# Expert units of the first table from 58 on: token halves side by side in 512-column products, summed by VectorE before the gelu

## What is computed

```
def peer_ffn(h, w_q, sub_keys, u_tab, v_tab):
    ...
    def expert_chunk(args):
        hx, ix, gx = args
        u = u_tab[ix]
        act = jax.nn.gelu(jnp.einsum('chkd,cd->chk', u, hx).astype(jnp.float32))
        vv = v_tab[ix]
        return jnp.einsum('chk,chkd->cd', (gx * act).astype(vv.dtype), vv)
```

## Time and profile before

| what | us |
|---|---|
| median of 3 runs | 2144.68 |
| the profiled execution, own time | 2145.49 |
| its span | 2144.2 |
| PE busy (share of the span) | 2113.1 (99%) |
| DVE busy | 1395.7 (65%) |
| ACT busy | 1247.4 (58%) |
| POOL busy | 977.1 (46%) |
| first table on PE, first and last start | 357.0 to 786.9 |

### The profile page before, as it was taken

One profiled execution on the slowest core, in us unless ns is written; L12 is line 12 of the kernel. 1 busy time (PEld: TensorE's weight loads), 2 busy tenths in 40 slices (PEclk: granted clock), 3 DMA queues, 4 the chain that ended last, 5 costly groups with the idle time before them and its releaser, 6 DMA issues.

```text
span 2144.2 us, 37243 instructions
## 1 busy us (share of the span) xinstructions
PE 2113.1 (99%) x14292; PEld 1958.1 (91%) x14292; DVE 1395.7 (65%) x2706; ACT 1247.4 (58%) x2272; POOL 977.1 (46%) x791
## 2 busy tenths in 40 slices
PE   7999999999999999999999999999999999999999
PEld 7999989999999998888889899998888999998887
DVE  4467655998676756666667765557764864757874
ACT  5669454546777865455445465746555465756553
POOL 4776557999667650000004785660001876661000
PEclk9999999999999999999999999999999999999999
DMA  6444565655444456666665554555565645455565
GB/s 231 149 138 129 172 197 173 196 178 180 145 140 147 141 168 204 195 192 192 195 195 196 186 157 139 155 180 167 187 205 158 189 146 168 141 165 177 187 194 160
DMA packets 103952, 370.59 MB, mean 173 GB/s; under 512 B 11480, under 2 KB 12896, under 8 KB 103264
## 3 DMA queue, kind: packets, MB, share of 16 engines
q1 hardware_dynamic: 103776, 368.21, 54.8%
HBM read 366.05 MB, written 2.11 MB: 172 GB/s over the span
## 4 chain that ended last, share of the span: by engine, by line
PE 88%; DVE 6%; ACT 2%; POOL 1%; issue 1%; DMA 1%; SPq 0%; DVEq 0%; ACTq 0%; POOLq 0%
PE stream_bank L568 14%; PE stream_bank L570 14%; PE stream_bank L569 14%; PE side_bank L568 9%; PE side_bank L570 9%; PE side_bank L569 9%; PE side_bank L577 4%; PE stream_bank L577 4%; PE side_bank L574 2%; PE stream_bank L574 2%; PE side_bank L918 1%; PE side_bank L917 1%; POOL unit_lo L2606 1%; ACT unit_hi L1181 1%; PE side_bank L746 1%
## 5 line engine op out<-in xcount | busy, mean ns | idle before, releaser
L2606 POOL TENSOR_TENSOR unit_lo<-raw,unit_hi 128x512 fp32r<-128x512 f32 (+1 forms) x724 | 938.5, 1324 | 943.6 <-ACT unit_hi L1181 941.6
L1181 ACT ACTIVATE unit_hi<-raw 128x1024 fp32r<-128x1024 f32 (+1 forms) x678 | 708.9, 1046 | 199.5 <-PE side_bank L570 66.0
L1777 DVE TENSOR_TENSOR unit_lo<-raw,unit_hi 128x1024 fp32r<-128x1024 f32 (+1 forms) x316 | 390.3, 1236 | 227.9 <-ACT unit_hi L1181 225.9
L568 PE MATMUL stream_bank<-hT,unit_hi 128*128 128x256 f32 x1360 | 398.9, 293 | 1.8 <-POOL unit_lo L2606 1.8
L570 PE MATMUL stream_bank<-hT,unit_lo 128*128 128x256 f32 x1360 | 384.6, 283 | 0.0
L569 PE MATMUL stream_bank<-hT,unit_hi 128*128 128x256 f32 x1360 | 384.5, 283 | 0.0
L568 PE MATMUL stream_bank<-h2T,unit_hi 128*128 128x256 f32 x1024 | 293.3, 286 | 0.0
L570 PE MATMUL stream_bank<-h2T,unit_lo 128*128 128x256 f32 x1024 | 289.8, 283 | 0.0
L569 PE MATMUL stream_bank<-h2T,unit_hi 128*128 128x256 f32 x1024 | 289.6, 283 | 0.0
L568 PEld LDWEIGHTS stream_bank<-hT,unit_hi 128*128 128x128 f32 x1360 | 259.9, 191 | 3.6 <-POOL unit_lo L2606 2.0
L569 PEld LDWEIGHTS stream_bank<-hT,unit_hi 128*128 128x128 f32 x1360 | 260.0, 191 | 1.6
(11 more groups left out here) (392 smaller groups left out, 4303.9 us busy)
## 6 DMA issues: line engine op xcount, KB each, us to landing
raw<-in_peer_u_dram SPq DMA_DIRECT2D x128, 512.0 KB, 3.5
raw<-in_peer_v_dram SPq DMA_DIRECT2D x128, 512.0 KB, 4.1
raw<-in_gate_dram SPq DMA_DIRECT2D x64, 512.0 KB, 3.5
raw<-in_gt_dram SPq DMA_DIRECT2D x44, 512.0 KB, 3.5
raw<-in_up_dram SPq DMA_DIRECT2D x44, 512.0 KB, 3.5
raw<-in_ffn_out_dram SPq DMA_DIRECT2D x44, 512.0 KB, 3.5
raw<-in_branch_dram SPq DMA_DIRECT2D x32, 512.0 KB, 3.5
raw<-in_w_gate_dram SPq DMA_DIRECT2D x24, 512.0 KB, 3.5
```

What stands on the lines that cost most here:

```text
L568: mm(out, l.hi, r.hi, start=start, stop=False)
L1181: activation(k.unit_hi[n % SPLIT_SLOTS][:, 0:w], k.raw[n % RAW_SLOTS][:, 0:w], ACT.Copy).then_inc(k.sem("unit_hi"), 1)
L1777: V.tensor_tensor(k.unit_lo[s][:, 0:w], k.raw[n % RAW_SLOTS][:, 0:w], k.unit_hi[s][:, 0:w], ALU.subtract).then_inc(unit_lo, 1)
L2606: last = G.tensor_tensor(k.unit_lo[s][:, cols], k.raw[n % RAW_SLOTS][:, cols], k.unit_hi[s][:, cols], ALU.subtract)
```

## The change

Units 58 to 127 of the first table go through `halves_unit`: 8 products of 512 and 8 of 256 columns. DVE has a new step `sum_unit(r)`: a reduce that reads the 512 columns of the stream bank in pairs (column t and 256+t), writes the 256 sums to the right half of the side bank `SIDE + 2 + r % 2`, and frees the stream bank. ACT's gelu of such a unit waits for this sum instead of PE and reads it; a new semaphore `unit_gelu` tells DVE that it is done. DVE's step r is put in another order: `sum_unit(r-1)`, `second_keys` of both halves, `gate_unit(r-1)`, `apply_gates`.

```diff
--- before.py
+++ after.py
@@ -172,6 +172,7 @@
 SETS, GROUP = 3, 4
 GROUPS = TOKENS // GROUP
 GATES_FROM, GATES_OVER = 55, 70
+HALVES_FROM = 58
 SLOTS_EXP, SLOTS_TURN = (21, 46), (28, 54)
 HEADS_MIXER = MEM_HEADS + Q_HEADS
 TOKEN_MAJOR = ("vm", "va", "w_out", "peer_v", "rv", "gv", "sv", "ffn_out")
@@ -922,7 +923,10 @@
         pe.wait_ge(k.sem("landed_sub_keys"), 16)
         scores(0)
         for r in range(KEYS):
-            fm_unit("peer_u", r, k.h2T, KD, ready=(lambda c: (k.sem("scaled_lo"), c // 2 + 1)) if r == 0 else None)
+            if r >= HALVES_FROM:
+                halves_unit("peer_u", r, k.h2T)
+            else:
+                fm_unit("peer_u", r, k.h2T, KD, ready=(lambda c: (k.sem("scaled_lo"), c // 2 + 1)) if r == 0 else None)
             if r == 1:
                 scores(1)
             if r in SLOTS_TURN:
@@ -1465,15 +1469,19 @@
         def evict_gated(r):
 
             b, m = k.bank_of["peer_u", r], tokens_gated(r)
-            act.wait_ge(unit_mm, U["peer_u", r] + 1)
+            src, done = k.bank[b][:, 0:TOKENS], k.free[b]
+            if r < HALVES_FROM:
+                act.wait_ge(unit_mm, U["peer_u", r] + 1)
+            else:
+                act.wait_ge(*k.over["peer_u", r])
+                src, done = k.bank[SIDE + 2 + r % 2][:, TOKENS:], k.sem("unit_gelu")
             if m:
                 if units_gated(r) > 2:
                     act.wait_ge(k.sem("unit_gated"), units_gated(r) - 2)
-                last = activation(k.bank[SIDE + 2 + r % 2][:, 0:m], k.bank[b][:, 0:m],
-                                  ACT.Gelu_apprx_tanh)
+                last = activation(k.bank[SIDE + 2 + r % 2][:, 0:m], src[:, 0:m], ACT.Gelu_apprx_tanh)
             if m < TOKENS:
-                last = activation(k.experts[:, r, m:], k.bank[b][:, m:TOKENS], ACT.Gelu_apprx_tanh)
-            last.then_inc(k.free[b], 1)
+                last = activation(k.experts[:, r, m:], src[:, m:], ACT.Gelu_apprx_tanh)
+            last.then_inc(done, 1)
 
         def expert_hi(j):
             if j == 0:
@@ -2218,13 +2226,16 @@
                                               k.slot_T[:, 2:4, t:t + 1].to_broadcast([P, 2, P]), ALU.is_equal, ALU.mult)
             last.then_inc(k.sem("second_hot"), 1)
 
+        def gelu_done(r):
+            return k.over["peer_u", r] if r < HALVES_FROM else (k.sem("unit_gelu"), r - HALVES_FROM + 1)
+
         def apply_gates(g, r):
 
             tokens = slice(g * GROUP, (g + 1) * GROUP)
             gates = k.bank[SIDE + g % 2][:, :].rearrange("p (t j) -> p j t", t=GROUP)
             dve.wait_ge(k.sem("gates_mm"), 2 * g + 2)
             V.tensor_copy(k.experts[:, r:, tokens], gates[:, r:, :])
-            dve.wait_ge(*k.over["peer_u", r - 1])
+            dve.wait_ge(*gelu_done(r - 1))
             V.tensor_tensor(k.experts[:, 0:r, tokens], k.experts[:, 0:r, tokens], gates[:, 0:r, :], ALU.mult).then_inc(
                 k.free[SIDE + g % 2], 1)
 
@@ -2233,7 +2244,7 @@
             if m == 0:
                 return
             row = k.experts[:, r, 0:m]
-            dve.wait_ge(*k.over["peer_u", r])
+            dve.wait_ge(*gelu_done(r))
             dve.wait_ge(*k.over["gates", m // GROUP - 1])
             V.tensor_tensor(row, row, k.bank[SIDE + 2 + r % 2][:, 0:m], ALU.mult).then_inc(
                 k.sem("unit_gated"), 1)
@@ -2250,15 +2261,24 @@
             cols = slice(t * P, (t + 1) * P)
             dve.wait_ge(*k.over["slots", t])
             own.then(V.tensor_tensor(k.slot_T[:, 3, cols], k.slot_T[:, 2, cols], k.gate_hi[:, cols], ALU.subtract))
+        def sum_unit(r):
+            b = k.bank_of["peer_u", r]
+            dve.wait_ge(unit_mm, U["peer_u", r] + 1)
+            V.tensor_reduce(k.bank[SIDE + 2 + r % 2][:, TOKENS:], k.bank[b][:, :].rearrange("p (a t) -> p t a", a=2), AXIS_X,
+                            ALU.add).then_inc(k.free[b], 1)
+
         for r in range(KEYS):
             advance("peer_u", r)
+            if r > HALVES_FROM:
+                sum_unit(r - 1)
+            for g in groups_built(r):
+                second_keys(g, 0)
+                second_keys(g, 1)
             if r:
                 gate_unit(r - 1)
             for g in groups_built(r - 2):
                 apply_gates(g, r)
-            for g in groups_built(r):
-                second_keys(g, 0)
-                second_keys(g, 1)
+        sum_unit(KEYS - 1)
         expert_lo(0)
         gate_unit(KEYS - 1)
         expert_lo(1)
```

## The result

The changed kernel takes 2147.32 us (median of 20 runs, 2144.68 to 2151.22) against 2142.66 us of the kernel before in the same series (20 runs, 2139.11 to 2147.41). The ratio is 1.0020, 95% interval 1.0014 to 1.0026: slower by 0.2%, 3.0 to 5.6 us. The forecast was +5.8 us (1.0027), 2150.5 us for the median, in a range of 2142.5 to 2160.

A forecast was written before the change was run, and what follows sets the result against it. PE bounds the kernel now; with the change a two-round loop through DVE and ACT was to decide. 61 x 0.11 = +6.7, 9 x -0.07 = -0.6, gaps -0.5, end +0.2: +5.8 us, median 2150.5 us, range 2142.5 to 2160.

The forecast's parts named there:

- 70 x 0.07 = 4.9 us: PE, units 58 to 127: each goes from 2.88 to 2.81 us, 4.9 us less if PE stays the bound.
- The reduce, 0.68: DVE, one reduce of 512 PSUM elements per unit: 0.68 us, from a 683 ns row; at the other end 1568 ns.
- The loop, 3.87 in the middle: Chain through PE, DVE and ACT over two rounds: 7.74 us, 3.87 a round; 3.83 early, 3.95 late.
- The gelu link: ACT, inside the loop: the gelu's two pieces, from start to the start of what follows, 0.39 us.
- The hand-over to PE: From the end of ACT's first keys to a waiting PE: 0.10 us, with 0.05 and 0.35 as ends.
- The sum, +5.8 us: Whole kernel: 61 units with a group +6.7, nine without -0.6, gaps -0.5, table's end +0.2.
- The end of the table, +0.2: Unit 127's reduce between PE's last product and the second table: +0.2 us, of at most 0.7.
- Stalls of 0.1 to 0.6 us in the waits: Sign in PE's waits: first keys (L1466) named on the gates' second half, several tens of times, 0.1 to 0.6 us each.
- The first, that all of PE's gain comes through: Rival: the loop stays shorter than PE's own round, under 3.70; 4.9 us gained less 0.2, 2140.0 us; chance 0.13.
- The second, a loop that is about even: Rival: a reduce of 0.60 and hand-overs of nothing take 0.12 off a round; 2143 to 2149 us; chance 0.23.
- a reduce of 1.0 us: Rival, DVE becomes the bound: 10 us more, 2160; chance 0.14 shared with a hand-over of 0.35, 2158.
- a PE unit that isn't shortened: Rival: PE's units gain nothing as 128-column products follow each; some 2 us more, inside the forecast's spread; no chance given.

The follow-up runs named there:

- the first experiment: The changed kernel with DVE's gate_unit and apply_gates moved between the second keys of half 0 and half 1: 2139.24 us, 0.9982 of the kernel before.
- the first two experiments: The changed kernel with gate_unit and apply_gates ahead of half 1's second keys on DVE, or half 1's first keys ahead of the gelu on ACT: 0.9982 and 0.9984.
- the reduce twice: The changed kernel with the reduce done twice in each unit, the second behind the first: 2171.25 us, 1.0131 of the kernel before.
- the reduce in the old order: The changed kernel with DVE's order of before behind the reduce, second keys of both halves last: 2148.43 us, 1.0029 of the kernel before.
- the reduce alone: The changed kernel with the old products (24 of 256 columns) in all units, the reduce reading the left half twice: 2150.65 us, 1.0036 of the kernel before.
- the order alone: The kernel before with only DVE's new order, second keys of both halves ahead of the gated rows, no reduce: 2142.89 us, 0.9999 of the kernel before.
- PE's part alone: The kernel before with units 58 to 127 as halves products, no reduce, the gelu reading the left half alone: 2137.71 us, 0.9975 of the kernel before.
- the last version: The changed kernel with gates ahead on DVE, first keys ahead on ACT, and unit 127 with old products and no reduce: 2135.91 us, 0.9973 of before.
- the second experiment: The changed kernel with the first keys of half 1 moved ahead of the gelu on ACT: 2139.81 us, 0.9984 of the kernel before.

## Why the prediction was right, and where its sizes were off

- **What bounds the kernel, and the mechanism.** Right. PE alone was the bound, and the loop half 0, second keys, gated rows, reduce, gelu, first keys, half 1 took its place. Taking the loop apart at either end gave 8.7 us back; the reduce without the products kept it; the order without the reduce had none of it. The stream of weights, which I cost at nothing, stayed covered: no view of PE's waits names a low part.
- **The term "70 x 0.07 = 4.9 us".** Measured alone 5.5 (0.079 a unit). The figures of the Trainium skill, "TensorE: Matmul & The Clock Gate", section "Wait — 56ns, not 53.3ns?", had given an estimate of 1.4; the interval of the run, 3.2 to 7.7 us less, leaves that out too.
- **The reduce, 0.68.** 0.693, with 691 to 700 ns over 70 of them. Its upper end, 1568 ns, was not near.
- **The loop, 3.87 in the middle.** It is 3.85. The passage above gives 0.04 + 1.05 + 0.82 + 0.73 (reduce and hand-over) + 0.33 + 0.75 + 0.07 = 3.79 from half 0 to the next half 1, where I had 3.87. The gelu link was mis-sized: 0.39 was read to the start of first keys that themselves had waited for PE's half 0; from the gelu's start to the next start it is 0.33. The hand-over to PE takes 0.05 to 0.07 after a short stall, not 0.10. PE's part, from half 1 at 623.44 over one unit to the modelled end of the next half 0 (627.08 + 0.27 = 627.35), is 3.91 where I had 3.87; with the loop cut, in the first experiment, the same stretch takes 3.84 to 3.88. This lengthening, about 0.04 us a round, is what the 8.7 us hold beside the late starts of 6.5 us; its cause isn't shown. 3.79 + 3.91 = 7.70 for two rounds, 3.85 each.
- **The sum, +5.8 us.** This is the step that was off: the stage gave 3.2, the runs 3.0 to 5.6. I counted 61 units with a group and 9 without, with six gaps, and six is also what the description of the kernel before says; the program leaves out five units (66, 78, 89, 101, 113), so they are 62 and 8. With these counts my prices give 62 x 3.77 + 8 x 2.88 = 256.8 us for the old stage (it is 257.0) and 62 x 3.88 + 8 x 2.81 - 0.5 = 262.5 for the new one (it is 260.2). Of the 2.3 us, 1.9 are the round, 3.85 instead of 3.88. The rest is the lead that the loop gets at each of the five gaps, larger than the 0.5 us in all that I gave: 62 x 3.85 + 8 x 2.80 = 261.1 against 260.2 measured.
- **The end of the table, +0.2.** In the changed kernel's profile PE stood 1.95 us there, 0.1 less than before; in the first two experiments 2.83, 0.8 more. See the last section.
- **Stalls of 0.1 to 0.6 us in the waits.** The stalls are there, nearly every second round, most of them 0.16 to 0.36 us long; but as waits the view shows only six, since modelled ends hide the rest. What I named as the sign of the theory was nearly absent in that view, and was found in the starts.
- **The rivals.** The first, that all of PE's gain comes through, is what the kernel does once the loop is cut; the change itself was 8.7 us away from it. The second, a loop that is about even, had 2143 to 2149 us, and the measured 2147.32 lies in that band and not in the forecast's 2149 to 2156. That is partly since the kernel before itself measured 2142.66 over 20 runs, 2.0 less than the three that I started from. Its mechanism, a reduce of 0.60 and hand-overs of nothing, isn't what the trace shows (0.69, and 0.03 to 0.07). DVE was not the bound in the change (42.13 of 50 us). In the old order it was, by way of a wait I had not named in the prediction. Two side sums of the prediction are off by themselves and decide nothing: with a reduce of 1.0 us DVE's own work would be 3.6 to 3.8 a round by its rows, not 3.7 to 3.9, and a PE unit that isn't shortened costs 61 x 0.035 + 9 x 0.07 = 2.8 us more, not 2.

## What to carry to other kernels

A step that fits an engine's free time can still cost, if it puts that engine's queue between a product and something that the same products need later: add up the loop through all queues from start to start and compare it with the round of the bound, before comparing busy times. Such a loop is cut by letting a step that could already run go ahead of one that waits inside the loop; it worked here at two links, on DVE and on ACT. Where products overlap in a profile, short stalls are seen in the starts and not in the view of waits.

## What was not expected of the hardware

- At the start of the second table PE has stood idle for 1.6 to 3.6 us, and the clock behind that differs between executions. Windows of PE from 790 to 800 us, before and with the change (stretch, length, busy with its count, granted clock, DMA share, GB/s):

```profile
790.00:800.00 10.00, 10.00 (x40) 0.87 0.60 204
```
```profile
790.00:800.00 10.00, 10.00 (x46) 1.00 0.78 256
```

  Before, PE's products run at the half level (1.2 GHz) behind an idle time of 2.05 us, with starts 0.43 us apart from 789.83 to 792.39 and 0.23 after 792.76; with the change, behind 1.95 us, at the full level. Of the other profiles those with 2.8 us and more (the first two experiments, the reduce twice with 3.55, the reduce in the old order, the reduce alone) granted half the clock behind it, the order alone did with 2.05 us, and those with 2.12 and 1.6 us (PE's part alone, the last version) kept it. Eight starts 0.2 us further apart are about 1.5 us (with the reduce twice it was more, some 14 starts), which is part of why single spans compare badly here.
- The same DVE instruction at that place, a subtract of 256 columns with both sources in SBUF, took 0.87 us before, 0.41 with the change and 1.49 in the first experiment:

```profile
787.70 0.87 DVE L2244 TENSOR_TENSOR expert_pair<-experts,expert_pair 128x256 fp32r<-128x256 f32 x1 [2.50 <-ACT expert_pair L1228]
...
787.03 1.26 POOL L2606 TENSOR_TENSOR unit_lo<-raw,unit_hi 128x512 fp32r<-128x512 f32 x1
```
```profile
788.24 0.41 DVE L2255 TENSOR_TENSOR expert_pair<-experts,expert_pair 128x256 fp32r<-128x256 f32 x1
...
788.24 1.54 POOL L2626 TENSOR_TENSOR unit_lo<-raw,unit_hi 128x512 fp32r<-128x512 f32 x1
```
```profile
779.51 1.49 DVE L2255 TENSOR_TENSOR expert_pair<-experts,expert_pair 128x256 fp32r<-128x256 f32 x1
...
779.46 1.26 POOL L2627 TENSOR_TENSOR unit_lo<-raw,unit_hi 128x512 fp32r<-128x512 f32 x1
```

  (Each fence holds DVE's row and then POOL's, before, with the change, and in the first experiment.) POOL is at its subtract of 512 columns at the same place. Before, POOL's starts first, at 787.03, and ends at 788.29; DVE's, begun at 787.70, ends 0.28 us behind it. In the first experiment POOL's ends at 780.72 and DVE's again 0.28 behind it, at 781.00. With the change the two start together, DVE's takes 0.41 and POOL's 1.54 instead of 1.26: there it is POOL that waits. The Trainium skill, "SBUF — State Buffer", section "SBUF: two separate sides", describes this: a DVE instruction with two SBUF inputs and a GpSimd one that reads SBUF contend for a shared pair of ports; whichever starts first has it for the whole instruction, and the other is blocked. These rows agree in that the two don't overlap freely; no experiment here moved POOL's instruction alone, so the cause isn't shown by a run. It fits that DVE's last steps at the table's end came up to 1.1 us later (1.49 against 0.41; it took 1.49 in the second experiment, too), and PE, which waits for that chain, stood there for 2.83 us in both experiments and 1.95 with the change.
